# Phase boundaries, first attention and semaphore clearing of a three-block transformer kernel

## What is computed

```python
# blocks 1 and 2 (l = 0, 1); m = six modulation vectors from silu(c) @ mod_w[l]
h = modulate(rms(x), m0, m1)
o = even_mixer(h)            # l = 0: gated linear attention and a softmax attention
o = odd_mixer(h)             # l = 1: gated recurrence (hgrn)
x = x + m2 * rms(o @ w_out)
x = x + m5 * rms(swiglu(modulate(rms(x), m3, m4)))
...
# the softmax attention of l = 0
qa, ka = rms(aq), rms(ak)    # 8 query heads, 2 key heads of 64
q, k = rope(qa), rope(ka)    # latents see 768 keys, the context 256
p = softmax(q @ k.T * 64 ** -0.5); b = p @ v
...
# block 3: delta rule and low-rank attention (mla) side by side, then 16 experts
branch_a, branch_b = deltanet(h), mla(h)
x = x + m2 * ((gates * branches) @ w_o)
x = x + m5 * experts(router_top(h))
```

## Time and profile before

| | us |
|---|---|
| median of 3 runs | 4721.04 (4717.77 to 4725.54) |
| the profiled execution, its own time | 4724.04 |
| its span in the profile | 4722.3 |
| att, begin of the clears before it to those behind it | 317 to 563 |
| out and ffn_up of block 1 | 563 to 1092 |
| in | 3143 to 3326 |
| mla | 3326 to 3740 |
| wo, then constants and route | 3870 to 4013 |
| experts | 4013 to 4722 |

### The profile page before, as it was taken

One profiled execution on the slowest core, in us unless ns is written; L12 is line 12 of the kernel. 1 busy time (PEld: TensorE's weight loads), 2 busy tenths in 40 slices (PEclk: granted clock), 3 DMA queues, 4 the chain that ended last, 5 costly groups with the idle time before them and its releaser, 6 DMA issues. The chain is left out here.

```text
span 4722.3 us, 48436 instructions
## 1 busy us (share of the span) xinstructions
PE 4163.0 (88%) x19557; PEld 2646.3 (56%) x19557; DVE 1475.4 (31%) x2739; ACT 879.8 (19%) x1705; POOL 596.4 (13%) x395
## 2 busy tenths in 40 slices
PE   6987779999979997899888999869898896999988
PEld 3654435557856765588776777644444443433332
DVE  2246332321013454433115666620123223011111
ACT  3223220000023333100013333310012201000000
POOL 0002102220001011132003333300002200000000
PEclk8988899999989999899989999979888896999999
DMA  4116411112011101343310100012200212799998
GB/s 156 36 63 217 161 36 54 54 54 87 25 54 41 48 29 55 125 172 114 117 32 25 29 23 12 5 66 91 79 0 0 113 71 88 304 404 400 411 410 355
DMA packets 323061, 545.19 MB, mean 115 GB/s; under 512 B 54956, under 2 KB 203148, under 8 KB 322200
## 3 DMA queue, kind: packets, MB, share of 16 engines
q1 hardware_dynamic: 322840, 542.10, 31.1%
HBM read 531.41 MB, written 10.63 MB: 115 GB/s over the span
## 5 line engine op out<-in xcount | busy, mean ns | idle before, releaser
L421 PE MATMUL ffn_down_ps<-ffn_down_w,ffn_hid 128*128 128x256 f32 x1760 | 387.4, 383 | 27.5 <-DMA ffn_down_w<-in_ffn_w_down 27.5
L421 PEld LDWEIGHTS ffn_down_ps<-ffn_down_w,ffn_hid 128*128 128x128 f32 x1760 | 337.8, 192 | 75.0 <-DMA ffn_down_w<-in_ffn_w_down 28.4
L2512 PE MATMUL dn_ps<-room,dn_w 128*128 128x512 f32 (+1 forms) x640 | 232.0, 517 | 4.8 <-DVE dn_qx L2983 2.4
L725 PE MATMUL ffn_up_ps<-room,ffn_up_w 128*128 128x384 f32 (+1 forms) x704 | 208.4, 440 | 19.9 <-DMA ffn_up_w<-in_ffn_w_gate 19.9
L725 PE MATMUL ffn_up_ps<-ffn_up_t,room 128*128 128x384 f32 (+1 forms) x704 | 205.0, 434 | 0.0
L725 PE MATMUL ffn_up_ps<-room 128*128 128x384 f32 (+1 forms) x704 | 203.9, 432 | 0.0
L3976 PE MATMUL experts_ps<-experts_ring,experts_xs 128*64 128x512 f32 (+1 forms) x768 | 169.6, 595 | 27.2 <-DMA experts_ring<-in_w_up 27.2
L145 PE MATMUL in_ps<-in_w,room 128*128 128x512 f32 x384 | 167.4, 599 | 14.4 <-DMA in_w<-in_w_in 14.4
L725 PEld LDWEIGHTS ffn_up_ps<-room,ffn_up_w 128*128 128x128 f32 x704 | 134.6, 193 | 78.9 <-DMA ffn_up_w<-in_ffn_w_gate 20.7
L3976 PE MATMUL experts_ps<-experts_ring,room 128*64 128x512 f32 (+1 forms) x768 | 163.3, 579 | 14.0 <-DMA experts_ring<-in_w_up 13.3
L1974 PE MATMUL hgrn_ps<-room,hgrn_w 128*128 128x512 f32 x384 | 174.4, 594 | 0.0
(11 more groups left out here) (588 smaller groups left out, 6554.7 us busy)
## 6 DMA issues: line engine op xcount, KB each, us to landing
experts_ring<-in_w_gate SPq DMA_DIRECT2D x128, 704.0 KB, 11.5
experts_ring<-in_w_up SPq DMA_DIRECT2D x128, 704.0 KB, 12.9
experts_ring<-in_w_down SPq DMA_DIRECT2D x160, 512.0 KB, 8.1
att_wm<-in_mod_w SPq DMA_DIRECT2D x20, 2048.0 KB, 8.8
ffn_up_wm<-in_ada_w SPq DMA_DIRECT2D x12, 2048.0 KB, 12.4
ffn_up_w<-in_ffn_w_gate SPq DMA_DIRECT2D x22, 1024.0 KB, 5.4
ffn_up_w<-in_ffn_w_up SPq DMA_DIRECT2D x22, 1024.0 KB, 7.6
ffn_down_w<-in_ffn_w_down SPq DMA_DIRECT2D x16, 1408.0 KB, 9.5
```

The lines of the kernel that those rows point to most:

```text
L421: mm = nc.tensor.matmul(ps[:, u % BANKS, 0:wd], xT[:, k, t * P - token0:(t + 1) * P - token0], wt[:, j % ring, k, 0:wd], start=k == 0, sto ...
L725: mm = nc.tensor.matmul(result(n, p), lhs[:, k, :], rhs[:, k, :], start=k == 0, stop=k == half - 1)
L2512: mm = nc.tensor.matmul(out, wt[:, h % 2, piece, k, :], hT[:, k, tok], start=k == 0, stop=k == KD - 1)
```

## The change

- `clear_all` clears each run of consecutive semaphore numbers with one instruction, in place of one per semaphore. In the new program 40 such instructions stand where 581 stood.
- `linear`, `closing`: the first block of weights comes in smaller pieces (a first one of one k-slice, or two of 22), each with a semaphore.
- `closing`: with kt 8 PE turns the tile two behind, not one.
- `gate_up`: the first quarter comes as `lo` and `hi`; the modulation products end two blocks earlier.
- `even_attention`: `two` is loaded first and alone gates the sums; the other constants gate what follows; the modulation biases are loaded behind the first two weights; ACT copies all three jobs, job 1 goes to bank 7; in the last pair the modulation products come at 0, 1, 2, 3.
- `odd_mixer`: the four loads of `bnd` come behind the first weights.
- `mla`: its input weights are loaded by `linear`, into a room that both phases share; the constants gate PE only behind the eight first products. One clear and one barrier are added behind mla.
- The two phases of constants are gone; `route` loads them behind `route_w`.

```diff
+def clear_all(nc, sems):
+    numbers = sorted(sem.num for sem in sems)
+    first = 0
+    for n in range(1, len(numbers) + 1):
+        if n == len(numbers) or numbers[n] != numbers[n - 1] + 1:
+            nc.sync.sem_clear(range(numbers[first], numbers[n - 1] + 1))
+            first = n
...
# linear
+                    if j + part == 0:
+                        sp.dma_start(wt[:, 0, 0:1, 0:wd], v[:, 0:1, c:c + wd]).then_inc(S["first_in"], 16)
+                        k0 = 1
...
+            then(sp)
...
# closing
+        firsts = ((0, 1), (1, 4), (4, 8)) if kt == KD else ((0, 2), (2, 6), (6, 11), (11, 22))
+        behind = 2 if kt == KD else 1
...
-                    if j == blocks - 1 and i:
-                        turn(tiles[i - 1])
-            turn(tiles[-1])
+                    if j == blocks - 1 and i >= behind:
+                        turn(tiles[i - behind])
+            for t in tiles[-behind:]:
+                turn(t)
...
# gate_up
-        take = -(-left // (blocks - b))
+        take = -(-left // max(blocks - 2 - b, 1))
...
+                if b == 0:
+                    sp.dma_start(wt[:, 0, 0, lo, :], views[0][:, lo, 0:width]).then_inc(S["lo_in"], 16)
+                    sp.dma_start(wt[:, 0, 0, hi, :], views[0][:, hi, 0:width]).then_inc(S["w_in"][0], 16)
...
# even_attention
+        return (0, 1, 3, 4) if j + 1 < PAIRS else (0, 1, 2, 3)
...
-            pe.wait_ge(S["const_in"], CONSTS)
+            pe.wait_ge(S["two_in"], 16)
...
-                if n:
-                    on = jobs[n - 1][2]
-                    pe.wait_ge(S[f"{on}_taken"], (dve_jobs if on == "dve" else act_jobs)[n - 1])
+                if m == 0 and u:
+                    pe.wait_ge(S["taken"], jobs_through[u - 1])
+                if m == 1:
+                    other_free(u)
+                if m == 2:
+                    pe.wait_ge(S["taken"], n - 1)
...
+                if t >= CTX_TILES:
+                    pe.wait_ge(S["taken"], jobs_of[u][1] + 1)
...
# mla
-            pe.wait_ge(S["const_in"], CONSTS)
             for u in range(8):
                 project(u)
+            pe.wait_ge(S["const_in"], CONSTS)
```

More of the change, by code:

```diff
@@ L45, in phase @@
             yield block, sems
-        for sem in every:
-            nc.sync.sem_clear(sem)
+        clear_all(nc, every)
         nc.all_engine_barrier()
+def clear_all(nc, sems):
[5 more added lines that the diff above has]
+            first = n
 class Steps:
@@ L97, in columns, with linear @@
     return [(v, c, min(width, end - c), [(t, min(width, end - c)) for t in tiles]) for c in range(first, end, width)]
-def linear(nc, tag, xT, kt, jobs, out, function, width=512, ring=3):
+def linear(nc, tag, xT, kt, jobs, out, function, then, width=512, ring=3):
     jobs = list(jobs)
@@ L109, in linear @@
         nc.psum_tensor(f"{tag}_ps", [P, 8, 512], F32) as ps,
-        phase(nc, tag, f"w_in*{2 * ring}", "mm_done", "taken", "stored*2") as (block, S),
+        phase(nc, tag, f"w_in*{2 * ring}", "first_in", "mm_done", "taken", "stored*2") as (block, S),
     ):
@@ L363, in weights @@
                         sp.dma_start(wt[parts_, j % ring, k0:k1, 0:wd], src[:, :, c:c + wd]).then_inc(S["w_in"][2 * (j % ring) + part], 16)
-            weights(0)
+            v, c, wd, _ = jobs[0]
+            for n, (k0, k1) in enumerate(firsts):
+                part = k0 >= kt // 2
+                at = halves[part][0] if type(v) is tuple else 0
+                for parts_, src in v[part] if type(v) is tuple else ((slice(0, P), v),):
+                    sp.dma_start(wt[parts_, 0, k0:k1, 0:wd], src[:, k0 - at:k1 - at, c:c + wd]).then_inc(S["first_in"][n], 16)
             if readout is not None:
@@ L1560, in qk, with other_free @@
                         mm.then_inc(S["scores"], 1)
+            def other_free(u):
+                j, at = divmod(u, TILES)
+                if at == 0 and j:
+                    pe.wait_ge(S["stored"], 2 * j)
+                mods_before = OPENING + LOOP * j + sum(x < at for x in mod_at(j))
+                pe.wait_ge(S["mod_out"], mods_before)
+                if at == 3 and j + 1 < PAIRS:
+                    pe.wait_ge(S["roped"], j + 3)
             def turn(u, n):
@@ L1585, in values @@
                     pe.wait_ge(S["stored"], 2 * j)
-                pe.wait_ge(S["mod_out"], OPENING + LOOP * j + (3 if lat else 4))
+                if not lat:
+                    pe.wait_ge(S["stored"], 2 * j + 1)
+                pe.wait_ge(S["mod_out"], OPENING + LOOP * j + sum(x < (LAT_UNITS if lat else TILES) for x in mod_at(j)))
                 n_keys = TILES if lat else CTX_TILES
@@ L1923, in _ @@
         def _(sp):
-            for d in range(2):
-                for layer in range(2):
-                    sp.dma_start(bnd[:, d, layer, :], bounds[d, layer].rearrange("(h p) -> p h", p=P), allow_slow_non_contiguous=True).then_inc(S["const_in"], 16)
             heads_v = w_in[:, 0:3 * D].rearrange("(p k) (s h c) -> s h p k c", p=P, s=3, h=H)
@@ L1939, in _ @@
                     sp.dma_start(wt[:, s, :, 0:b - a], flat_v[:, :, at + a:at + b]).then_inc(S["w_in"][s], 16)
+                if j == 0:
+                    for d in range(2):
+                        for layer in range(2):
+                            sp.dma_start(bnd[:, d, layer, :], bounds[d, layer].rearrange("(h p) -> p h", p=P), allow_slow_non_contiguous=True).then_inc(S["const_in"], 16)
         arrived, per_slot = [], [0] * ring
@@ L3138, in project @@
                 if u == 0:
-                    pe.wait_ge(S["w_in"], 64)
+                    pe.wait_ge(latents_in[0], 16 * 3)
+                if what == "cq" and n == 0:
+                    pe.wait_ge(latents_in[1], 16)
                 for k in range(KD):
@@ L4164, in mixture @@
                 ring, load, piece_in, room, (xs_even, xs_odd[:, :, :]), hid, hidT, out)
-        for sem in piece_in:
-            nc.sync.sem_clear(sem)
+        clear_all(nc, piece_in)
         nc.all_engine_barrier()
```

144 lines of the change are left out of this document (79 added, 65 removed).

## The result

| | before | changed |
|---|---|---|
| median, us | 4721.50 (4717.77 to 4725.54, 4 runs) | 4611.82 (4602.04 to 4615.73, 4 runs) |
| ratio | | 0.9764, 95% interval 0.9747 to 0.9782 |
| profiled execution, us | 4724.0, span 4722.3 | 4610.79, span 4608.8 |

The kernel became 110 us faster; the forecast was 4608, and two more sets of runs of the changed kernel gave 4610.36 and 4611.80. The sum of terms (113.3) can be held against the two profiled executions, whose spans differ by 113.5.

A forecast was written before the change was run, and what follows sets the result against it. PE, busy 88% of the span, was taken as the bound in most phases. Terms summed to 113.3 us; 4724.0 less 113.3 is 4610.7, less 3.0 for the profiled run 4608. Range 4584 to 4640; own case 4600 to 4616, 60%.

The forecast's parts named there:

- Clears: Phase boundaries: 581 single semaphore clears taking 35.9 us become 40 range clears taking 2.4, so 33.0 us less.
- Attention's prologue: Start of attention: sums wait only for `two`, modulation weights are issued earlier, first scores at +38.5 not +45.5: 7.0 us less.
- Pairs: Attention's pairs: PE's waits before turned jobs 1 and 2 go, 3.84 us a pair, 11.5 in the first three.
- the clock: Rival, 18%: granted clock recovers with the waits gone, some 8 us in attention's pairs and 3 in out: 4597 us.
- Last pair and end: Attention's fourth pair gains 1.5 us of waits; earlier modulation product and stores gain 6.5 at the end.
- Turning two behind: Closings: PE's waits before turned tiles go, 8.1 us in out, 2.7 in the second out, 1.3 in wo.
- First pieces: Closings: smaller first weight loads let PE start earlier, 1.5 us each in out and wo, 3.0 in each ffn_down.
- ffn_up: ffn_up: earlier first product gains 0.9 and 0.4 us, stores hidden behind the second one 6.6: 7.9 less.
- mla: mla's start: with weights loaded earlier and constants waited for later, PE starts at once: 14.7 us less.
- The range cost: Rival, 7%: a range clear costs what its semaphores cost singly, so clears gain nothing: 4641 us.
- the slower outcome: Rival, 2%: range clears cost much per semaphore at every boundary; at 0.25 us each the kernel takes 4751 us.
- Late copies: Rival, 12%: ACT copies attention's job 0 late at each unit, the pairs' gain is lost: 4621 us, or 4633.

The follow-up runs named there:

- the experiment: The changed kernel with the tiles of all closings turned one behind again, first pieces kept: 4630.48 against 4611.80 us; wo took 77.6, 4.9 more.
- a_oldmla: The changed kernel with mla's start wholly as before (weights loaded in mla, PE waiting for all four loads and all constants): 4625.39 us, 13.6 slower; mla 414.4.

## Why the prediction was right, and where its terms were not

The time, 4611.8, lies in the forecast's own case, 4600 to 4616, and the mechanisms are those named. That the sum of terms comes within 0.2 us of the two profiled executions is luck in part: by the table the attention, the turned tiles and the rest gave some 9 us more than their terms, and ffn_down, experts, mla, ffn_up, the clears and route some 9 less.

- **Clears** (33.0): 32.5. The lower bound was taken, rightly: 31 to 107 ns an instruction. The count was 588 and not 581, since seven more clears stood at the end of experts.
- **Attention's prologue** (7.0): 6.1. The sums start at +1.8 (forecast +2.1), load 2 ends at +30.2 (+29.1); the scores come 0.9 later than forecast, with that load. The step that slipped is the first load of modulation weights: it was issued at +5.3 as forecast but landed 11.5 later and not 9.6, so product 0 ended at +20.4 and not at +19.6.
- **Pairs** (11.5 in three, 3.84 each): 17.0, 13.5 and 12.7 in the three profiles. The waits themselves are 10.2, a little less than forecast; the new wait costs 0.24 in the row shown and not the 0.1 to 0.15 assumed. What was mis-sized is that the clock was put in a rival and not in the term: 2.5 to 6.8 us of it came along each time (PE busy 110.9 before, then 104.1, 107.7 and 108.4). The second pair, for which 44.8 was forecast against 48.6, took 43.3, 44.2 and 44.2, and no wait stands before the second half of L1629's row.
- **Last pair and end** (1.5 + 6.5 = 8.0): 10.2 from the last pair's first transpose to the clears. Undoing the end's part cost 7.2, against 6.5 forecast. Clears start 0.3 behind ACT's last copy, as said.
- **Turning two behind** (8.1 + 2.7 + 1.3 = 12.1): 18.7. Three steps failed. The wait before the last turn but one was said to give nothing, and shrank from 2.69 to 1.81 in both outs. In wo one wait of 1.62 was counted where its last tiles have two. And all products were taken at 7.03, when in the kernel before one of the last in each out took 8.73 and 8.19 (granted clock 0.80 and 0.86). With these three the rows of the kernel before and of the change give 10.7 in out, 4.8 in the second out and 2.2 in wo, 17.7 in all.
- **First pieces** (1.5 in each of out and wo, 3.0 in each ffn_down): in ffn_down 2.7 and 1.5. The second is the larger miss: PE starts 4.3 behind the first issue there, not 3.2, because the piece landed 4.3 behind its issue where the first ffn_down's was there after 2.6. The Trainium skill, DMA: Bandwidth & Descriptors, Anatomy of one DMA, from which the prediction took another 2.6, gives its figures for DMAs that GpSimd issues. Here SP issues all of them, and one of the two pieces agrees with that 2.6. Out's total of 12.3 less the 10.7 of turning leaves 1.6 for its pieces; wo's (3.4 less 2.2, or less the 4.9 of the experiment) can't be told from what a phase varies.
- **ffn_up** (7.9): 7.3. **hgrn and in** (4.2): 4.4. **route** (5.9): 5.6.
- **mla** (14.7): 13.0, or 13.7 against a_oldmla. The start itself moved by 14.7, as forecast; what failed is that the rest of the phase was taken as unchanged. The small products some 55 us in run at a lower clock now, and the phase gives 2 us back.
- **Rivals.** The range cost and the slower outcome are out by the 107 ns. Late copies are out: one bank with ACT alone is 8 us better than DVE's share. The clock did come back, 2.5 to 6.8 us in the pairs and up to 1.7 in each out, where 8 and 3 had been counted, and it was hidden in the total by ffn_down (4.5 short in the table, 2.7 of it the short last tiles in the profile of before), by mla (1.7) and by experts (2.0). What is open is what decides in which execution the clock falls; no run here tells that.

## What to carry to other kernels

Before pricing an edit from one profile, look how much its phase varies by itself, above all where short waits lie between products: a second profile of the same kernel costs less than an explanation of 3 us. Compare the idle and the busy time of the engine apart: here the idle time of three pairs repeated within 0.2 us over ten profiles, and all the variation was in the busy time. A wait of 2 to 3 us before each of many products costs its own length and some of the product behind it, so an edit that removes such waits should be priced with both; and when it pays in one caller, try it in the others (here 12 and 4 us more in ffn_down). Where an engine waits for several loads, list them all before pricing the removal of one: at mla's start the constants held PE as long as the weights.

## What the runs showed of the hardware

- A clear of a run of semaphores takes 31 to 107 ns; single ones came every 0.06 us. At the 17 boundaries that both kernels have, 35.7 us of standing still for all engines became 3.2.
- The same code of the same kernel at the same place shows a granted clock of 0.91 and 0.92 in two executions and 0.94 and 0.89 in two of its earlier form, with 58.6 to 62.0 us for it. Where the waits of 2.48 between them were gone, the products took 9.66 in both executions.
- Over the three pairs of the attention the same 1183 matmuls kept PE busy for 104.1 to 105.0 us in five executions and for 107.6 to 108.6 in five others, with idle time of 27.9 to 28.1 in all ten.
- At mla's start 37 small matmuls took 4.96 us at a granted clock of 1.00 in the kernel before, and 6.68 at 0.69 in the changed one.
- Experts, where the DMA share is 0.93, took 704.7 to 711.4 us over 14 profiles, in no order with the kernels.
